# Chunk 0 and the low-rank chunk of each layer from the unnormalised input, with the per-token factor applied when they are evacuated

## What is computed

```python
def rmsnorm(x, w):
    y = xf * lax.rsqrt(jnp.mean(xf * xf, axis=-1, keepdims=True) + EPS)
    return (y * w.astype(jnp.float32)).astype(x.dtype)
...
h = rmsnorm(x, p['norm_w'])
proj = jnp.einsum('bld,dn->bln', h, p['w_in']).astype(f32)      # D_MODEL = 1024 in, 3088 out
...
g_gla = jax.nn.log_sigmoid(jnp.einsum('blr,rn->bln', gla_lr, p['gla_w_gate_up']) + p['gla_b_gate']) / GLA_TAU
...
return x + out, states
```

## Time and profile before

| | us |
|---|---|
| median of three runs | 351.10 |
| the three runs | 351.09, 351.10, 353.65 |
| the profiled execution | 353.67 |
| its span, first to last instruction | 351.8 |
| around the span | 1.9 |

### The profile page before, as it was taken

The page is one execution under the profiler, slowest core; times in us unless marked ns, Lnnn a source line. Parts: engine busy times, 40 slices in busy tenths (PEclk is TensorE's granted clock), DMA queues, the critical chain, the costliest instruction groups (busy, mean ns, idle before and its releaser), DMA issues.

```text
span 351.8 us, 6392 instructions
## 1 busy us (share of the span) xinstructions
PE 330.3 (94%) x2546; PEld 280.9 (80%) x2546; DVE 236.1 (67%) x501; ACT 121.0 (34%) x262; POOL 43.4 (12%) x81
## 2 busy tenths in 40 slices
PE   7899998889999999989979999999999999989991
PEld 6688876667889898869967888887888989877990
DVE  2574499986628978485749727596644897686454
ACT  4243001150691003583412620115177010566321
POOL 4018530006000000250000000000600000120000
PEclk9999999999999999899999999999999999999997
DMA  8977622232531500799915472322262242476503
GB/s 281 380 258 229 241 95 86 61 109 72 163 111 61 180 2 2 240 199 273 351 39 159 141 268 91 119 80 102 92 182 64 102 136 66 124 192 120 184 1 123
DMA packets 28013, 50.85 MB, mean 145 GB/s; under 512 B 6288, under 2 KB 6864, under 8 KB 27984
## 3 DMA queue, kind: packets, MB, share of 16 engines
q1 hardware_dynamic: 25968, 44.06, 37.9%
q0 software_dynamic: 1728, 6.29, 7.5%
q10 hardware_dynamic: 288, 0.09, 0.1%
HBM read 46.80 MB, written 3.64 MB: 143 GB/s over the span
## 4 chain that ended last, share of the span: by engine, by line
PE 75%; DVE 13%; POOL 4%; ACT 4%; issue 2%; DMA 1%; DVEq 0%; POOLq 0%; ACTq 0%
PE pr L490 41%; PE pr L764 10%; DVE att L1327 2%; PE wk L557 2%; DVE h L1059 2%; PE wk L679 2%; PE wk L504 2%; PE wk L725 2%; POOL lev L1577 2%; PE wk L602 1%; POOL lev L1579 1%; PE wk L570 1%; DMA x<-in_xt 1%; PE wk L671 1%; PE wk L617 1%
## 5 line engine op out<-in xcount | busy, mean ns | idle before, releaser
L490 PE MATMUL pr<-h,wring 128*128 128x264 f32 x768 | 178.9, 389 | 3.2 <-DVE h L1059 3.2
L490 PEld LDWEIGHTS pr<-h,wring 128*128 128x128 f32 x768 | 143.3, 190 | 30.0 <-issue 5.9
L764 PE MATMUL pr<-a_hi,w_hi 128*128 128x264 f32 x96 | 27.6, 288 | 0.0
L764 PE MATMUL pr<-a_lo,w_hi 128*128 128x264 f32 x96 | 27.2, 283 | 0.0
L764 PE MATMUL pr<-a_hi,w_lo 128*128 128x264 f32 x96 | 27.2, 283 | 0.0
L877 ACT ACTIVATE v<-pr 128x264 f32<-128x264 f32 x12 | 4.7, 388 | 48.2 <-PE pr L490 48.2
L865 ACT ACTIVATE h<-x 128x264 f32<-128x264 f32 x24 | 9.5, 420 | 32.8 <-DVE x L1480 30.7
L948 ACT ACTIVATE zs<-pr 128x264 f32<-128x264 f32 x16 | 6.0, 384 | 41.7 <-PE pr L490 41.7
L1327 DVE COPY_PREDICATED att<-masks,wk 128x512 f32<-128x512 int32 x20 | 17.6, 950 | 1.0
L764 PEld LDWEIGHTS pr<-a_lo,w_hi 128*128 128x128 f32 x96 | 18.1, 188 | 0.1
L764 PEld LDWEIGHTS pr<-a_hi,w_hi 128*128 128x128 f32 x96 | 18.1, 188 | 0.1
(11 more groups left out here) (281 smaller groups left out, 539.6 us busy)
## 6 DMA issues: line engine op xcount, KB each, us to landing
wring<-in_w_in SPq DMA_DIRECT2D x100, 256.0 KB, 3.0
wring<-in_w_out SPq DMA_DIRECT2D x20, 256.0 KB, 3.7
w_hi<-in_w_out POOLq DMA_DIRECT2D x6, 512.0 KB, 4.3
w_lo<-in_w_out POOLq DMA_DIRECT2D x6, 512.0 KB, 7.8
x<-in_xt SPq DMA_DIRECT2D x2, 528.0 KB, 4.7
out_y<-h SPq DMA_DIRECT2D x4, 264.0 KB, 2.0
s5m_t<-in_s5m SPq DMA_DIRECT2D x2, 512.0 KB, 4.4
ss<-in_hg_in SPq DMA_DIRECT2D x2, 512.0 KB, 4.0
```

Of the source, the lines that this page charges most:

```text
L490: mm = nc.tensor.matmul(ring_bank(layer, i)[:, 0:TT], wring[:, slot, n, :], act_in[:, k, :], start=(k == 0), stop=(k == KT - 1))
L764: mm = nc.tensor.matmul(ring_bank(layer, i)[:, 0:TT], w[:, j % WSLOTS, n, :], a[:, k, :], start=(k == 0 and p == 0), stop=(k == KT - 1 and ...
```

## The change

`xw`, eight tiles that share the memory of `zs`, holds `x * w` without `rstd`. Chunk 0 and the low-rank chunk are computed from `xw`; VectorE evacuates both after `scale_x` with a multiplication by `rstd` (`first_chunks`), where ScalarE evacuated them before. The two have a semaphore of their own, `first_evac`, and `chunk_out` picks the right one for all who wait for a chunk. The matmuls of the mean square move from ahead of chunk 0 into it: behind k = 5 in layer 0, and behind k = 3 in layer 1. In layer 0, too, VectorE now adds the squared tiles, so that two matmuls are left. In layer 0 `xw[0..3]` are made by VectorE ahead of those sums and `xw[4..7]` by ScalarE behind its squares; for layer 1 VectorE makes each tile behind its `residual`. `s5_steps` no longer waits for the constants.

```diff
+FIRST = 2
+SUM_AT = (5, 3)
...
+        xw = zs
...
+            def project_first(layer):
+
+                ring_free(pe, layer, C_F0)
                 for k in range(KT):
-                    pe.wait_ge(sq_ready, k + 1)
-                    mm = nc.tensor.matmul(wk[:, 0, 0:TT], ones_d[:, :], h[:, k, :], start=(k == 0), stop=(k == KT - 1))
-                mm.then_inc(ms_done, 1)
+                    half, n = divmod(k, KH)
+                    if n == 0:
+                        slot = use[0] % RING
+                        pe.wait_ge(w_in_sem[slot], 16 * (use[0] // RING + 1))
+                        use[0] += 1
+                    scaled_by_weight(pe, layer, k)
+                    mm = nc.tensor.matmul(ring_bank(layer, C_F0)[:, 0:TT], wring[:, slot, n, :], xw[:, k, :],
+                                          start=(k == 0), stop=(k == KT - 1))
+                    if n == KH - 1:
+                        mm.then_inc(proj_done if half else half_done, 1)
+                    if k == SUM_AT[layer]:
+                        mean_square(layer)
...
@@ low-rank chunk @@
-                                              h[:, KH * half + n, :], start=(half == 0), stop=(half == 1))
+                                              xw[:, KH * half + n, :], start=(half == 0), stop=(half == 1))
...
@@ tensor @@
-                mean_square(layer)
                 for i in range(NCH - 1):
-                    if i == C_LR:
+                    if i == C_F0:
+                        project_first(layer)
+                    elif i == C_LR:
                         project_low_rank(layer)
...
@@ scalar: norm, gate_logs, main @@
+                if n == 0:
+                    act.wait_ge(par_in, 16)
+                    for k in range(KH, KT):
+                        step(fn(xw[:, k, :], x[:, k, :], ACT.Copy, scale=par(Q_NORM + k)), xw_act)
...
+                chunk_out(act, layer, C_F0)
...
-                evac(layer, C_F0, x3[:, 0, :])
-                evac(layer, C_LR, lr_t)
                 evac(layer, C_F1, x3[:, 1, :])
...
@@ vector @@
+            def scale_by_weight(layer, k):
+                if layer == 0 and k == 0:
+                    dve.wait_ge(x_in[0], 16)
+                step(ts(xw[:, k, :], x[:, k, :], par(Q_NORM + layer * KT + k), None, ALU.mult), xw_ready)
+
+            def first_chunks(layer):
+                for i, dst in ((C_F0, x3[:, 0, :]), (C_LR, lr_t)):
+                    dve.wait_ge(proj_done, layer * NCH + i + 1)
+                    step(tt(dst, ring_bank(layer, i)[:, 0:TT], rstd, ALU.mult), first_evac)
...
             dve.wait_ge(par_in, 16)
+            s5_steps()
+            for k in range(KH):
+                scale_by_weight(0, k)
+            for m in range(1, KT - 1):
+                sum_squares(0, m)
             dve.wait_ge(cst_in[0], 16)
-            s5_steps()
             for layer in range(DEPTH):
                 scale_x(layer, Q_NORM + layer * KT, h_ready)
+                first_chunks(layer)
                 if layer == 0:
                     lower_bounds()
...
                     residual(layer, m)
+                    if layer + 1 < DEPTH and m:
+                        settle()
+                        for k in range(m if m > 1 else 0, m + 1):
+                            scale_by_weight(layer + 1, k)
```

More of the change, by code:

```diff
@@ L267, in build @@
         sum_ready, diag_used = sem("sum_ready"), sem("diag_used")
+        xw_ready, xw_act, first_evac = (sem(n) for n in ("xw_ready", "xw_act", "first_evac"))
         half_done = sem("half_done")
@@ L327, in build, with chunk_out, scaled_by_weight @@
         USES = NCH + 2 + 6 + KT
+        def chunk_out(eng, layer, i):
+            if i < FIRST:
+                eng.wait_ge(first_evac, layer * FIRST + i + 1)
+            else:
+                eng.wait_ge(chunk_evac, layer * (NCH - FIRST) + i - FIRST + 1)
+        def scaled_by_weight(eng, layer, k):
+            if layer == 0 and k >= KH:
+                eng.wait_ge(xw_act, k - KH + 1)
+            else:
+                eng.wait_ge(xw_ready, (KH if layer else 0) + (layer - 1 if layer else 0) * KT + k + 1)
         BANK_TURN = list(range(NCH - 1)) + [NCH, NCH + 1, NCH - 1] + list(range(NCH + 2, USES))
@@ L339, in ring_free @@
             if i < NCH:
-                eng.wait_ge(chunk_evac, layer * NCH + i + 1)
+                chunk_out(eng, layer, i)
             elif i < NCH + 2:
@@ L435, in _ @@
                     if i == NCH - 4:
-                        sp.wait_ge(chunk_evac, layer * NCH + C_RV1 + 1)
+                        chunk_out(sp, layer, C_RV1)
                         sp.dma_start(vs[layer].rearrange("(t p) b -> p t b", p=P), v[:, :, TP:TT]).then_inc(vs_out, 16)
@@ L494, in mean_square @@
             def mean_square(n):
[L496 to L501, removed]
-                for k in range(KT):
-                    pe.wait_ge(sq_ready, k + 1)
-                    mm = nc.tensor.matmul(wk[:, 0, 0:TT], ones_d[:, :], h[:, k, :], start=(k == 0), stop=(k == KT - 1))
-                mm.then_inc(ms_done, 1)
+                pe.wait_ge(sum_ready, n + 1)
+                nc.tensor.matmul(wk[:, 0, 0:TT], ones_d[:, :], h[:, 0, :], start=True, stop=False)
+                pe.wait_ge(sq_ready, n * KT + KT)
+                nc.tensor.matmul(wk[:, 0, 0:TT], ones_d[:, :], h[:, KT - 1, :], start=False, stop=True).then_inc(ms_done, 1)
+            def project_first(layer):
+                ring_free(pe, layer, C_F0)
+                for k in range(KT):
+                    half, n = divmod(k, KH)
[10 more added lines that the diff above has]
+                        mean_square(layer)
             def project(layer, i):
-                product(layer, i, proj_done, 2 * layer if i == 0 else None)
+                product(layer, i, proj_done, 2 * layer if i == FIRST else None)
             def project_low_rank(layer):
@@ L518, in project_low_rank @@
                         mm = nc.tensor.matmul(ring_bank(layer, C_LR)[32 * n:32 * n + 32, 0:TT], wring[:, slot, n, 0:32],
-                                              h[:, KH * half + n, :], start=(half == 0), stop=(half == 1))
+                                              xw[:, KH * half + n, :], start=(half == 0), stop=(half == 1))
                     mm.then_inc(proj_done if half else half_done, 1)
             def low_rank(layer):
-                pe.wait_ge(chunk_evac, layer * NCH + C_LR + 1)
+                chunk_out(pe, layer, C_LR)
                 if layer == 0:
@@ L591, in level @@
                 if n == 0:
-                    pe.wait_ge(chunk_evac, layer * NCH + C_GK + 1)
+                    chunk_out(pe, layer, C_GK)
                 if n >= 2:
@@ L642, in rotate @@
             def rotate(layer):
-                pe.wait_ge(chunk_evac, layer * NCH + C_RK + 1)
+                chunk_out(pe, layer, C_RK)
                 pe.wait_ge(lvl_used, layer * NL + NL)
@@ L784, in _ @@
                             pe.wait_ge(cst_in[1], 16)
-                        pe.wait_ge(chunk_evac, layer * NCH + C_I1 + 1)
+                        chunk_out(pe, layer, C_I1)
                         turn(layer, 0, [v[:, t, P * b:P * b + P] for b in range(2) for t in range(2)])
                     if i == C_RQ:
-                        pe.wait_ge(chunk_evac, layer * NCH + C_GV1 + 1)
+                        chunk_out(pe, layer, C_GV1)
                         turn(layer, 1, [v[:, 2 + t, P * b:P * b + P] for b in range(2) for t in range(2)])
@@ L799, in _ @@
                     if i == C_U0:
-                        pe.wait_ge(chunk_evac, layer * NCH + C_RV1 + 1)
+                        chunk_out(pe, layer, C_RV1)
                         turn(layer, 4, [v[:, 4 + t, P * b:P * b + P] for b in range(2) for t in range(2)])
@@ L989, in _ @@
                 if layer == 0:
-                    act.wait_ge(par_in, 16)
                     act.wait_ge(cst_in[0], 16)
                     lower_bounds()
-                evac(layer, C_F0, x3[:, 0, :])
-                evac(layer, C_LR, lr_t)
                 evac(layer, C_F1, x3[:, 1, :])
@@ L1298, in level_operands @@
                     dve.wait_ge(eb_ready, layer * 2 + 1)
-                    dve.wait_ge(chunk_evac, layer * NCH + C_GQ + 1)
+                    chunk_out(dve, layer, C_GQ)
                     step(tt(qe[:, 0:2, :], q3[:, 0:2, 0:TP], eb[:, 0:2, 0:TP], ALU.mult))
@@ L1451, in head_gates @@
             def head_gates(layer, tiles):
-                dve.wait_ge(chunk_evac, layer * NCH + NP + 2 + tiles.stop)
+                chunk_out(dve, layer, NP + 1 + tiles.stop)
                 settle()
@@ L1480, in residual, with sum_squares @@
                 step(tt(x[:, m, :], x[:, m, :], ring_bank(layer, NCH + 8 + m)[:, 0:TT], ALU.add), out_used)
-            def sum_squares(layer, m):
-                dve.wait_ge(sq_ready, (layer + 1) * KT + m + 1)
+            def sum_squares(n, m):
+                dve.wait_ge(sq_ready, n * KT + m + 1)
                 settle()
@@ L1507, in _ @@
```

(10 more changed lines are left out.)

## The result

| | before | changed |
|---|---|---|
| median, 16 runs each, us | 351.35 | 353.76 |
| lowest and highest, us | 350.23, 356.83 | 352.23, 354.81 |
| profiled execution, us | 353.67 | 353.59 |
| its span, us | 351.8 | 351.7 |

The changed kernel takes 1.0057 times as long (95% interval 1.0030 to 1.0084). This ratio compares means and leaves out the three executions of the kernel before at 356.7 to 356.8 us, which belong to its slow state. The changed kernel is slower, by 0.6% where 1.4% was forecast. The two profiled executions are equally long. That is no contradiction: the profiled execution of the kernel before was one of its longer ones, that of the changed kernel was a usual one. The first experiment looks into that difference.

A forecast was written before the change was run, and what follows sets the result against it. Up to 72.29 us TensorE waits for VectorE's chain; between the layers TensorE itself sets the time. The sum 353.67 + 4.8 - 2.5 gave 356.0 us, expected of the median too, with a range of 353.0 to 358.2.

The forecast's parts named there:

- the first two rivals: Chunk 0 finds the clock high: 353.7 to 354.3 us, chance 0.13; the 2.57 us lie elsewhere: 353.4 us, chance 0.14.
- start of `scale_x`, layer 0: Layer 0's mean square stands behind 12 slow passes of chunk 0, so `scale_x` starts at 16.0, not 12.68: +3.3 us.
- two evacuations: Layer 0, behind `scale_x`: VectorE evacuates two chunks at 0.43 us each, less some overlap: +0.85 us.
- GpSimd's chain: Layer 0: GpSimd, `s5_coefficients` and the levels follow L1063's start, 4.2 us later, by as much; no change of length.
- level 1 at the low clock: Layer 0: TensorE's wait of 0.78 becomes some 6 us, bringing the clock down: +0.6 us, between nothing and 1.
- between the layers: TensorE goes on with chunk 0 without waiting, so `C_F1` of layer 1 starts at 185.66 instead of 188.14: -2.5 us.
- If the clock again rises 4.9 us after the dense passes begin: TensorE, layer 0's chunk 0: the clock rises at 13.6, just ahead of the mean square at 14.0.
- `gate`'s slack in layer 1: `gate` starts near 197.3; level 0's operands are done about 206.4, wanted at 207.7: the gain survives by 1.2 us.
- How the profile stands to the median: Early high clock makes the median before 2.57 us lower than the profile; the changed kernel's median stays at 356.0 us.
- the high clock in chunk 0: Rival, layer 0: the gap doesn't bring the clock down, `scale_x` at 14.4, result 353.7 to 354.3 us; chance 0.13.
- the lost gain of layer 1: Rival: VectorE late at level 0, or one more stretch at 0.50, giving 357.5 to 358.5 us; chance 0.10.
- The hidden delay: Rival: layer 0's delay is hidden as TensorE waits there anyway, giving 348.6 to 351.2 us; chance 0.05.

The follow-up runs named there:

- The first experiment: The kernel before, run once more with no edit: 352.14 us (350.39 to 357.18), its profiled execution 354.59 us.
- `gate_late`: The changed kernel with VectorE's `gate` of layer 0 held back until GpSimd's `accurate_sines` is done: 359.67 us in a single execution.
- `warm20`: The changed kernel with 20 instead of 7 warm-up matmuls on TensorE: 352.54 us.
- `sum3`: The changed kernel with layer 0's mean square behind k = 3 of chunk 0 instead of k = 5: 353.12 us.
- `before_again`: The kernel before, run once more with no edit: 352.14 us; its profiled execution, 354.59 us, has an early high clock.
- `layer0_only`: Layer 0 as in the changed kernel, layer 1 as in the kernel before: 357.77 us, ratio 1.0138 to the kernel before.
- `before_warm0`: The kernel before without its 7 warm-up matmuls: 353.86 us, ratio 1.0019 to the kernel before.
- `layer1_only_b`: Layer 0 as in the kernel before, layer 1 as in the changed one, second set of runs: 349.46 us, ratio 0.9876 to the kernel before.

## Why the prediction was partly wrong

The sign, the place of the gain and that of the loss were right, and 353.76 lies in the range of 353.0 to 358.2. The size was not: 356.0 is 2.2 us too much. That the range holds it is no merit of the sum: it lies at the low end, which was there for the first two rivals (353.7 to 354.3, and 353.4). The first is not what happened, and the runs speak against the second. By terms, from the two profiled executions:

| term | forecast, us | measured, us |
|---|---|---|
| start of `scale_x`, layer 0 | +3.3 | +2.70 (12.68 to 15.38) |
| two evacuations | +0.85 | +0.70 (15.91 to 19.31, less 2.70) |
| GpSimd's chain | 0 | -1.27 (15.47 to 14.20) |
| level 1 at the low clock | +0.6 | +0.38 (48.84 to 51.34, less 2.12) |
| between the layers | -2.5 | -2.58 (8.16 to 5.58) |
| sum | +2.3 | -0.1 |

Two operations of one line of GpSimd's chain, in the kernel before:

```profile
33.45 0.61 POOL L1577 TENSOR_SCALAR lev<-lev 128x160 f32<-128x160 f32 x1
34.76 0.93 POOL L1577 TENSOR_SCALAR lev<-lev 128x160 f32<-128x160 f32 x1
```

- **The missing term is GpSimd's chain.** "GpSimd, `s5_coefficients` and the levels follow by as much" was wrong: the chain was taken as a fixed length, though the trace of before had operations of one line at 0.61 and at 0.93 us (above). L1149's counterpart came only 2.1 us later, not 4.2, and 1.27 us of the difference are the chain. That alone is over half of the error. `gate_late` shows the cause.
- **The start of `scale_x` was mis-sized by 0.6.** The step was "If the clock again rises 4.9 us after the dense passes begin". In this execution the passes changed to 0.22 us at about 12.7, 4.2 us behind their start: they start 0.44 us apart up to 12.63 and 0.22 apart from 12.89 on. The rest of the step held: idle time, some 10 of the 12 passes at the low level, mean square behind them and not behind the sums. `warm20` and `sum3` bear on it from two sides.
- **Level 1** was right in kind (a wait of 4.74 us, then a stretch at 0.50, then 0.49 us of VectorE waiting) and 0.2 too large. The bound of `gate`'s slack in layer 1 was right: 1.7 us were left (208.34 to 210.06) where 1.2 were worked out.
- **How the profile stands to the median** was the step that kept the direction right. Compared with the profiled execution alone, the change would have been nothing. That TensorE may start the mean square at the high clock before, and not after the change, was argued from a difference of 2.57 us between runs; `before_again` shows such an execution, with `scale_x` at 10.20 where 10.2 was expected, and `layer0_only` shows the clock falling ahead of chunk 0. That this is what the usual executions do is likely and not shown, and the times of `before_warm0` speak against the warm-up burst being all that decides it.
- **Of the rivals**, the high clock in chunk 0 and the lost gain of layer 1 are out by the traces. The hidden delay is out by `layer0_only`, which is 1.4% slower than the kernel before. The second rival, the 2.57 us lying in a stretch at 0.50, gave 353.4, and the measured time is close to that. The equal mean granted clocks of the 351.1 and 353.7 us executions speak against it, so that is taken for chance, but no trace of a 351.1 us execution settles it.

## What to carry to other kernels

A product moved ahead of a wait gains only where its engine is what ends last: the same edit is worth 2.6 us between the layers and costs in layer 0, where VectorE's queue up to GpSimd's start counts. The edit puts two evacuations into it and 12 passes, most of them slow, ahead of the mean square that it waits for. Split such a change by place and try the halves, as the better kernel here was one half (0.988). When a kernel's times fall into groups, count the groups before a difference of medians is believed. And a serial chain on GpSimd has no fixed length: what VectorE does beside it counts.

## What the hardware showed that I had not expected

- GpSimd's elementwise operations take up to 2.3 times as long beside VectorE's: 0.45 us alone and 1.02 us in the kernel before for the same 128x160 product. The chain of 21 operations was seen at 13.56 (`gate_late`), 14.20 (the changed kernel), 14.56 (`layer1_only_b`) and 15.47 us (the kernel before) with the same work in it.
- The idle time between the layers costs more than itself in some executions: in `before_again` a stretch at 0.50 follows, and 16 passes take 5.49 us instead of 3.80.
- The granted clock's column reads 1.00 for the first 8 us of every trace here, also where the passes follow each other at 0.44 us. Only in `layer0_only` does it show the slow start of chunk 0 (0.52 from 8.3 to 11.6); in the changed kernel it reads 1.00 beside the same slow passes. At the start the durations of the passes have to be read, not the column.
